# One block for the output norm and the completion of the inverses, bonus loads spread over the chunk steps, and a projection that takes the attention rows first

## What is computed

```python
def encoder_layer(x, p, lambda_init):
    n = rms_norm(x, p['ln1_g'])
    proj = n @ p['w_in']
    rkv = centred_conv(proj[..., :c0], p['conv_rkv'])
    ya = rwkv7_mixer(n, r, k, v, p)              # 8 heads x 64, both directions
    yb = diff_attention(qd, kd, vd, p, lambda_init)  # 4 heads, v 128
    x = x + jnp.concatenate([ya, yb], axis=-1) @ p['w_out']
    n2 = rms_norm(x, p['ln2_g'])
    x = x + (jax.nn.silu(n2 @ p['w_gate']) * (n2 @ p['w_up'])) @ p['w_down']
    return x
# diff_attention ends in: o = rms_norm(o, p['subln_g']) * (1.0 - lambda_init)
# rwkv7_mixer ends in: out = (yn + bonus) * g, yn being y_sum with mean and variance taken per head
```

## Time and profile before

| | us |
|---|---|
| median of 3 runs | 2462.61 (2459.39 to 2468.22) |
| profiled execution, its device time | 2464.25 |
| its span in the profile | 2462.5 |
| TensorE busy | 2185.3 (89%) |
| VectorE busy | 1103.2 (45%) |
| ScalarE busy | 829.2 (34%) |
| GpSimd busy | 349.6 (14%) |

### The profile page before, as it was taken

One profiled execution on the slowest core, in us unless ns is written; L12 is line 12 of the kernel. 1 busy time (PEld: TensorE's weight loads), 2 busy tenths in 40 slices (PEclk: granted clock), 3 DMA queues, 4 the chain that ended last, 5 costly groups with the idle time before them and its releaser, 6 DMA issues. The chain is left out here.

```text
span 2462.5 us, 41471 instructions
## 1 busy us (share of the span) xinstructions
PE 2185.3 (89%) x17078; PEld 1851.3 (75%) x17078; DVE 1103.2 (45%) x1554; ACT 829.2 (34%) x1356; POOL 349.6 (14%) x366
## 2 busy tenths in 40 slices
PE   6999998867397888856999599999999999999999
PEld 5888883344386555546888288999998889999987
DVE  5433006579564777661767544232232222233221
ACT  6111114665374444433445322222222122222211
POOL 0000000000002998043445200000000000000000
PEclk9999999866567999966999799999999999999999
DMA  3222212135693000034784435322223332222232
GB/s 122 89 87 95 80 69 87 51 150 228 232 250 129 1 1 20 33 122 93 187 197 123 145 116 170 103 70 75 77 86 110 120 111 77 77 74 71 76 120 73
DMA packets 133539, 258.47 MB, mean 105 GB/s; under 512 B 10945, under 2 KB 80961, under 8 KB 132129
## 3 DMA queue, kind: packets, MB, share of 16 engines
q1 hardware_dynamic: 133408, 256.63, 32.5%
HBM read 184.69 MB, written 68.93 MB: 103 GB/s over the span
## 5 line engine op out<-in xcount | busy, mean ns | idle before, releaser
L210 PE MATMUL ff_acc<-normed_nh,normed_ff_low 128*128 128x320 f32 x1344 | 416.7, 310 | 6.3 <-SPq L158 5.1
L211 PE MATMUL ff_acc<-normed_nl,normed_ff_high 128*128 128x320 f32 x1344 | 416.3, 310 | 0.0
L212 PE MATMUL ff_acc<-normed_nh,normed_ff_high 128*128 128x320 f32 x1344 | 416.3, 310 | 0.0
L2636 DVE TENSOR_TENSOR normed_ff_low<-normed_ff_raw,normed_ff_high 128x1024 fp32r<-128x1024 f32 x126 | 154.3, 1225 | 427.7 <-ACT normed_ff_high L2600 427.6
L210 PEld LDWEIGHTS ff_acc<-normed_nh,normed_ff_low 128*128 128x128 f32 x1344 | 253.2, 188 | 7.0 <-SPq L158 5.4
L211 PEld LDWEIGHTS ff_acc<-normed_nl,normed_ff_high 128*128 128x128 f32 x1344 | 253.3, 188 | 0.0
L212 PEld LDWEIGHTS ff_acc<-normed_nh,normed_ff_high 128*128 128x128 f32 x1344 | 253.2, 188 | 0.0
L2600 ACT CAST normed_ff_high<-normed_ff_raw 128x1024 fp32r<-128x1024 f32 x126 | 131.8, 1046 | 234.5 <-PE ff_acc L212 233.8
L211 PE MATMUL ff_acc<-normed_ff_low,ff_hh 128*128 128x512 f32 x420 | 163.4, 389 | 0.0
L210 PE MATMUL ff_acc<-normed_ff_high,ff_hl 128*128 128x512 f32 x420 | 163.4, 389 | 0.0
L212 PE MATMUL ff_acc<-normed_ff_high,ff_hh 128*128 128x512 f32 x420 | 163.4, 389 | 0.0
(11 more groups left out here) (321 smaller groups left out, 4287.1 us busy)
## 6 DMA issues: line engine op xcount, KB each, us to landing
dram_sx<-pr_sx SPq DMA_DIRECT2D x8, 2816.0 KB, 8.1
ch_ops<-dram_sx SPq DMA_DIRECT2D x88, 256.0 KB, 4.8
normed_ff_raw<-in_w_gate SPq DMA_DIRECT2D x44, 512.0 KB, 3.3
normed_ff_raw<-in_w_up SPq DMA_DIRECT2D x44, 512.0 KB, 3.3
normed_ff_raw<-in_w_down SPq DMA_DIRECT2D x44, 512.0 KB, 3.6
pj_packed<-in_w_in SPq DMA_DIRECT2D x24, 512.0 KB, 4.5
heads_vt<-dram_sx SPq DMA_DIRECT2D x44, 256.0 KB, 5.4
dram_proj<-pj_mixed SPq DMA_DIRECT2D x12, 656.0 KB, 3.3
```

The costliest lines, as they stand in the source:

```text
L210: nc.tensor.matmul(out, ll, rh, start=start, stop=False)
L211: nc.tensor.matmul(out, lh, rl, start=False, stop=False)
L212: return nc.tensor.matmul(out, lh, rh, start=False, stop=stop)
L2636: nc.vector.tensor_tensor(low[s][:, :], raw[s], high[s][:, :].bitcast(F32), ALU.subtract).then_inc(cut_low[s], 1)
```

## The change

1. `attention_out` and `solve_out` become one block, `attention_out_and_solve_out`. Streams are interleaved: TensorE does a group's first products, a head's ten transposes, the group's second products. `half_ps` and `whole_ps` are single (two banks each), the transposes have three banks, single. The norm's small steps are done for all heads at once. Squares and transposed heads use the room of `y_last`; the attention's `o_rows` and two pairs of buffers of the stage before it lie in `y_first`.
2. The chunk stage's constants (masks, `same`, ident, decay) are loaded in that block, behind the inverses and ahead of the heads' stores. In the chunk stage GpSimd zeroes the state first and the operand slots after it, buffer by buffer; TensorE waits for the zeroing before the first three state products and not before the inner products; SP loads step 2 only after the first state products.
3. The eight bonus loads are issued one each at steps 5, 6, 9, 10, 13, 14, 15 and 16.
4. VectorE adds the bonus of the last three tiles of the mix. The stage doesn't wait for the landing of z; the semaphore lives on, and SP in the projection waits for it before it loads the z rows.
5. The projection loads the first tile's attention rows and its z rows separately, the weights in eight pieces of 512 KB, those for the attention rows first, and multiplies in that order.

```diff
 def attention_out_and_solve_out(nc, g):     # replaces attention_out and solve_out
+        half_ps, whole_ps = (c.ps(n, (P, 2 * 512)) for n in ("half_ps", "whole_ps"))
+        turn_ps = c.ps("turn_ps", (P, 3 * 512))
+        room = g.y_last[:, :, :, :].rearrange("p m e t -> p (m e t)")
+            def _(sp):
+                for grp in range(NG):
+                    sp.dma_start(inv[:, grp, :, :].rearrange("p i j -> p (i j)"),
+                                 g.inverses[:, grp * BLK * BLK:(grp + 1) * BLK * BLK]).then_inc(inv_in[grp], 16)
+                    for q in (1, 3):
+                        sp.dma_start(below[QUADS[q], grp, :, :].rearrange("p u c -> p (u c)"), g.below[q // 2, :, grp]
+                                     ).then_inc(below_in[grp], 16)
+                    if grp == 0:
+                        sp.dma_start(ident[:, :], g.small_of("ident")).then_inc(ident_in, 16)
...
+                for h in range(HEADS):
+                    sp.wait_ge(kept, h + 1)
+                    sp.dma_start(g.mix[RW + h * P:RW + (h + 1) * P, :], oT[h % 2]).then_inc(stored[h % 2], 16)
...
+                sp.wait_ge(chunk_consts, 112)
...
+                sum_up(0)
+                sum_up(1)
+                turn_inverse(0)
+                sum_up(2)
+                sum_up(3)
+                invert()
                 for h in range(HEADS):
+                    turn_inverse(h + 1)
+                    scale(h)
+                turn_inverse(NG - 1)
...
+                first(0)
+                second(0)
+                pe.wait_ge(ident_in, 16)
+                for h in range(HEADS):
+                    first(h + 1)
+                    turn_head(h)
                     if h + 1 < HEADS:
+                        second(h + 1)
+                second(NG - 2)
+                first(NG - 1)
+                second(NG - 1)
...
+                for h in range(HEADS):
+                    square(h)
+                keep_half(0)
+                root()
+                act.wait_ge(gained, 1)
+                keep_whole(0)
+                for h in range(HEADS):
+                    keep_half(h + 1)
+                    keep_head(h)
+                    if h + 1 < HEADS:
+                        keep_whole(h + 1)
+                keep_whole(NG - 2)
+                keep_half(NG - 1)
+                keep_whole(NG - 1)
 
 def chunks_and_mix(nc, g):
+    LATE = TILES - 3
+    BONUS_AT = (5, 6, 9, 10, 13, 14, 15, 16)
...
                 for n in (1, 2):
+                    if n == 2:
+                        for d in both:
+                            sp.wait_ge(bst_done[d], 1)
...
-                    if n == 3 * GS:
+                    if n in BONUS_AT:
+                        i = BONUS_AT.index(n)
+                        k = i // 2
                         for d in both:
-                            sp.wait_ge(u_done[d], n)
...
+                            sp.wait_ge(u_done[d], GS * min(k + 1, 3))
+                        row = (k % 2 * 2 + i % 2) * P + k // 2 * CH
+                        sp.dma_start(g.bon[HALVES[i % 2], k, :], g.bonus[row:row + CH, :]).then_inc(bonus_in, 16)
...
-                sp.wait_ge(stored, 16 * sum(len(runs) for _m, runs in GROUPS))
...
-                pe.wait_ge(zeroed, 1)
                 for p in range(PIECES):
                     inner_products(0, p)
                 for n in range(CHUNKS):
+                    if n < 3:
+                        pe.wait_ge(zeroed, n + 1)
...
-                pool.wait_ge(consts, 96)
                 for d in both:
                     scale_identity(d, 0)
+                for d in both:
+                    nc.gpsimd.memset(vs[0][CHAN[d], d, :, :], 0.0)
                 for s in range(3):
                     for d in both:
-                        nc.gpsimd.memset(ops[s][TOKS[d], :, R_AT[d], :], 0.0)
...
+                        last = nc.gpsimd.memset(ops[s][TOKS[d], :, R_AT[d], :], 0.0)
+                    last.then_inc(zeroed, 1)
...
+                for m in range(LATE, TILES):
+                    dve.wait_ge(gated_y, m + 1)
+                    at = two_chunks(m)
+                    tt(z[:, :, at, :], z[:, :, at, :], bonus[:, :, at, :], ALU.add).then_inc(done_late, 1)
 
 def out_project(nc, g):
+        ORDER = [(b, ks, ks + 2, q) for q, (b, lo) in enumerate(((0, HK), (1, HK), (0, 0), (1, 0))) for ks in (lo, lo + 2)]
...
+                load_m0(FROM_ATTENTION, m0_loaded)
+                weights_part(0)
+                weights_part(1)
                 sp.dma_start(ident[:, :], g.small_of("ident")).then_inc(weights, 16)
...
+                for w in range(2, 5):
+                    weights_part(w)
+                sp.wait_ge(g.z_stored, PRIMED + g.z_stores)
+                load_m0(FROM_Z, m_loaded[0])
+                for w in range(5, 8):
+                    weights_part(w)
                 load_m(1, 1)
```

More of the change, by code:

```diff
@@ L1330, in _ @@
                 total(FIRSTS - 1)
[L1331 removed]
+                for m in range(LATE):
                     pool.wait_ge(gated_y, m + 1)
@@ L2259, in turn @@
                     last.then_inc(turned, 1)
-                product(0, 0, 0, first=True)
+                first_product()
                 with pe.Fori(0, PAIRS - 1) as i:
```

425 lines of the change are left out of this document (201 added, 224 removed).

## The result

The changed kernel takes 2432.86 us (median of four executions, 2423.77 to 2435.84) against 2462.79 for the kernel before, a ratio of 0.987 with a 95% interval of 0.9844 to 0.9897. It is faster, by about 30 us. Two later comparisons of the same two kernels gave 0.9862 (0.9826 to 0.9898) and 0.9873 (0.985 to 0.9896), 34 and 31 us, so 30 to 34 us is what the three together say. The prediction was 2415, a gain of 47.4, and 2430 as the upper end: direction right, size too large, outside its range. The profiled execution took 2435.84 (span 2434.1), the longest of its four.

A forecast was written before the change was run, and what follows sets the result against it. TensorE's last stretch, 1423.7 to 2462.5, bounds the kernel; savings ahead come off one for one. 17.2 + 9.7 + 8.0 + 12.5 = 47.4 off 2464.25 gives 2416.9, as a median 2415 us; range 2405 to 2430.

The forecast's parts named there:

- Part A: Output norm and inverses merged in one block: 61.4 us against 78.6, -17.2, bounds -12.4 and -18.9.
- the 1.7 us for late code: Merged norm and inverses block: allowance for TensorE's code fetch stalls, taken as 1.7 us between bounds 0 and 6.5.
- Part B: Head of the chunk stage, constants and zeroing moved ahead: TensorE starts at 6.1 us instead of 15.8, -9.7.
- Covered, by 1.1; if it isn't, 1 to 2 us: Early chunk steps: held loads land at 21.8 us, wanted at 22.9; if late, 1 to 2 us lost.
- Part C: Chunk steps, bonus loads one a step: -8 us, bounds all 9.1 back or only 5.
- It fits, narrowly, at the four steps that also move y: Chunk steps: a bonus load brings DMA work to 8.1 of 8.4 us, 0.96 of the step.
- Part D: Mix to projection: first DMA 6.0 us earlier, then 6.5 saved to the end of the first product, together -12.5.
- It doesn't do what it says: Rival: a wait for stores or constants still ends last, so the head or projection change gives little; 2426, chance 0.05.
- The long steps were not the bonus loads': Rival, chunk steps: two of three long steps might be code fetch, so spreading gives 1 us; 2422, chance 0.07.
- The bonus spread saturates each step: Rival, chunk steps: operands come late at all eight bonus steps, costing 58 us; slower at 2472, chance 0.02.
- The clock in the first product: Rival, projection: clock stays low, first product runs at half clock, 8.1 us more; 2423, chance 0.10.
- The merged block was not serial: Denies a rival: norm and inverses copies and bursts wait for each other, merging worth only 5 us; 2427, chance 0.10.

The follow-up runs named there:

- its two variants above: Kernel before with only the bonus loads spread one a step, ratio 0.9974; kernel before with only the third step's loads held until the first state products, 1.0019.

## Why the prediction was wrong, point by point

Means over profiles: the kernel before and its two variants above, and the changed kernel with every variant that leaves the stretch alone (for the chunk steps its three profiles and the one with the identity later, against the two of the kernel before).

**What bounds the kernel**: right. 1038.80 us of the end are unchanged.

**Part A** (-17.2, bounds -12.4 and -18.9): the two blocks together took 77.2 to 78.6, the merged one 59.5 to 64.6, on average 63.1 over thirteen profiles: -14.8, within the bounds and 2.4 short. Order and starting point came as worked out; TensorE begins 6.5 us in:

```profile
1064.99 3.62 PE L2067 MATMUL as_half_ps<-as_by_col,as_below 32*32 32x32 f32 x128 [7.08 <-DVE as_by_col L2023]
...
1074.14 0.21 PE L2081 MATMUL as_whole_ps<-as_by_row,as_half 32*32 32x32 f32 x1 [1.24 <-issue]
...
1080.98 1.75 PE L2067 MATMUL as_half_ps<-as_by_col,as_below 32*32 32x32 f32 x58 [3.40 <-issue]
...
1107.20 2.66 PE L2067 MATMUL as_half_ps<-as_by_col,as_below 32*32 32x32 f32 x92 [1.09 <-issue]
```

The step that failed is the 1.7 us for late code, "nearer to none, because TensorE now pauses for data where it used to pause for code". The three waits above are 5.7, and at 3.40 one is longer than the 2.79 of the earlier trace rows; over the thirteen profiles such waits are 4.3 to 9.4 us, 6.4 on average. The pauses for data, 2.2 at most, didn't hide them. The block's own bound of 6.5 was the better value. With it the sum would have been too long, so its other terms had some 3 us too much. They price every burst at the half clock of the earlier trace rows; the granted clock in the merged block was 0.53 to 0.65, and the shortest block had the 0.65.

**Part B** (-9.7): the head took 21.4 to 22.3 and takes 12.5 to 13.6, -8.6 on average. The first inner product came 7.0 us after the stage's start in the first profile, and the forecast was 6.1. Behind it stands the step that cost more. "Covered, by 1.1; if it isn't, 1 to 2 us" asked only whether the held loads bring the *operands* in time, and they did: no wait for an operand stands in the first steps. It was not asked what those loads do to the code packets. The earlier trace rows had already shown such a stall. The first two intervals went from 16.7 to 20.5 to 22.3, +4.8 on average, 2.7 of it shown to be the hold's. By the traces the 4.8 are 3.1 us of waits for nothing and 1.6 of half clock behind them (3.1, 0, 1.7 and 1.6 in the four profiles, counted as half of the time that TensorE worked at 0.50); with the hold in the old kernel it is 2.5 and none. Why the half clock follows in three of these profiles and not in the fourth, whose stop was the 2.93, stays open. The stretch of that step in the first profile:

```profile
1144.58:1158.64 14.06, 11.42 (x191) 10.22 (x193) 6.57 (x21) 4.35 (x12) 4.21 (x5) 0.76 0.92 175
```

0.76 of the full clock on average, 1.00 in the second profile of the same kernel, where the interval took 11.86.

**Part C** (-8, bounds -9.1 and -5): measured alone, -6.4 (-3.5 to -9.4) in time and -3 to -4.5 in the steps; in the changed kernel 4 to 7 against the batch. The reading of the earlier trace rows was right: the batch made those steps long. The term that was mis-sized is "It fits, narrowly, at the four steps that also move y". A share of 0.96 worked out as a mean didn't mean 0.96 in each step. Two intervals of the changed kernel with one load each:

```profile
1202.87:1212.12 9.25, 8.65 (x192) 7.70 (x193) 6.57 (x21) 4.26 (x12) 4.22 (x5) 1.00 1.09 219
1239.10:1248.51 9.41, 8.64 (x193) 7.61 (x193) 6.58 (x21) 4.36 (x12) 4.23 (x5) 1.00 1.08 220
```

1.09 and 1.08, not 0.95 at most, as the change's sign was to be. The first is followed by the 1.47 us stop. Where the same loads stand at steps without y, the excess is 4.5 to 6.4 in three profiles and not 7.3 to 10.4. The reason taken for the near end of the range, "three steps of operands are held ahead", protects against late operands and says nothing of code.

In the nineteen intervals as a whole the changed kernel (mean 168.7 of four profiles) gained 1.9 on the kernel before (170.7) where 8 was due. 3.7 was the spread's worth in the old kernel, so some 2 more are lost between the parts; the batch too is dearer in the changed kernel, 174.3 against 170.7. That the code's place against the loads shifts with every change ahead of it would do this. It was not tested by itself, and the cause of these 2 us stays open.

**Part D** (-12.5): the first DMA came 5.6 us earlier after the last step's products (6.0 forecast), and from there to the next stage it is 160.5 to 161.7 in place of 166.3, -5.1 (6.5 forecast). Together -10.7. The rows landed as worked out, the attention rows 3.0 after the first DMA (2.8), the first piece at 4.3 (4.2):

```profile
1373.36 0.38 SPq L2205 DMA_DIRECT2D op_m<-dram_mix  x1
...
1376.36 0.62 ACT L2329 CAST op_m_high<-op_m 128x512 fp32r<-128x512 f32 x1 [14.53 <-DMA op_m<-dram_mix]
...
1377.67 1.04 ACT L2325 CAST op_w_high<-normed_ff_raw 128x1024 fp32r<-128x1024 f32 x1 [0.69 <-DMA normed_ff_raw<-in_w_out]
...
1381.30 1.04 ACT L2325 CAST op_w_high<-normed_ff_raw 128x1024 fp32r<-128x1024 f32 x1 [2.59 <-DMA normed_ff_raw<-in_w_out]
...
1381.53 0.80 PE L210 MATMUL op_acc<-op_w_high,op_m_low 128*128 128x512 f32 x1 [17.55 <-DMA op_ident<-in_small]
```

What failed is "the pieces come every 1.35 us": the second came 3.6 after the first. The identity, whose load moved from first to fourth of the queue, held the product back to 8.2, a wait that the prediction overlooked; the experiment shows that it costs nothing, as the second piece is later still.

**Sum**: -14.8 -8.6 +2.9 (steps) -10.7 = -31.2, beside 30 to 34 measured. Short of the forecast are 2.4 + 1.1 + 10.9 + 1.8 = 16.2, two thirds of them in the chunk steps. These exceed 21 times 8.42 by 13.4 us: 8.5 of waits for nothing, 2.4 of half clock behind them and 2.5 of other. In the kernel before it was 10.5: 7.4, 2.2 and 0.9. The forecast took 8 of these away; the change left as much late code as it found. The step that failed is thus the one behind both B and C: loads held back or spread were priced by whether their operands come in time and whether a mean share stays under 1, and what they do to TensorE's code was put at nothing.

The bounds of the range don't add up as stated: the four terms above the forecast (+4.8, +2.4, +3 and 3.4 for D's start) give 2429, without the last 2425, and not 2424.

**Rivals.** "It doesn't do what it says" falls. "The long steps were not the bonus loads'" named the code as the cause in place of the loads; the runs show both in one, code made late by the loads. "The bonus spread saturates each step" was given 0.02 as a loss of 58 us: the share did pass 1.0 at two or three of the eight, at less than a tenth of that price, because TensorE there waited for one packet of code and not for its operands. The clock in the first product was 0.80 and not low throughout. The merged block was not serial. No rival had code made late by the change's own loads, though a row of late code stood in part A; that is why the range ended at 2430.

The Trainium skill (Runtime: NRT & Kernel Launch, Instruction fetch mechanics) says that code is streamed in blocks of 16 KB by a DMA queue and that crossing a block is mostly hidden. The size agrees with the trace (94 packets, 1.54 MB), and so does "mostly": 34 packets in the chunk steps left ten waits or fewer. As a rule to plan with it doesn't hold beside full queues, where single waits came to 3.8 us.

## What to carry to other kernels

Loads that bring every operand in time can still make an engine's code late; look for waits that end by nothing shown, in the middle of a run of equal instructions, and for the distance of the packets in the instruction queue. Before loads are moved or spread, write down the DMA share of each step that they go to and not a mean: here loads of 1.6 us cost nothing that shows at shares of 0.6 to 0.7 and 2 to 5 us in all where they took some steps over 1. When several parts of a change fill idle time of the same resource, don't add up their gains unchecked: here the spread was worth 3.7 us by itself in the later steps, which gained 1.9 with the whole change.

An edit that moves loads to other steps of a queue's program need not move them so in time. The loads written for steps 18, 19 and 20 all left together, because SyncE's queue first waits for the buffer of the last operand loads, three steps ahead, and after that the loads' own waits were met or nearly so. The trace shows it and the edit doesn't.

## What the runs showed of the hardware that was not expected

A wait for code follows the loads to wherever they are put: 3.57 us at the batch's place, 3.77 with the batch at the end of the steps, 1.6 to 2.9 for the longest where held loads meet the second step, and 4.9 us in all when fewer loads are let go at once.

Such a stop is often paid for twice. Of 23 stops of 1.8 to 3.8 us inside the steps of the 17 profiles, 18 were followed by 3.4 or 6.8 us at a granted clock of 0.50.

VectorE was slowed in the merged block, where GpSimd copies in SBUF beside it. Three of four scalings of the same shape took longer, 1.82 to 2.10 us in all thirteen profiles with this block, than the 1.43 to 1.49 of the kernel before, whose norm had no GpSimd work beside it; the transposes between them, with one input, did not. VectorE and then GpSimd, of the changed kernel:

```profile
1075.03 1.45 DVE L2042 TENSOR_TENSOR first_y_first<-first_y_first,as_st 128x1280 f32<-128x1280 f32 x1
...
1078.18 1.91 DVE L2024 STREAM_TRANSPOSE as_by_row<-as_inv 128x1024 f32<-128x1024 f32 x1
1079.94 2.01 DVE L2042 TENSOR_TENSOR first_y_first<-first_y_first,as_st 128x1280 f32<-128x1280 f32 x1
...
1085.55 1.88 DVE L2042 TENSOR_TENSOR first_y_first<-first_y_first,as_st 128x1280 f32<-128x1280 f32 x1
```
```profile
1078.50 2.12 POOL L2013 COPY rows_est<-as_by_row 32x1024 f32<-32x1024 f32 x2
1080.67 3.25 POOL L2013 COPY rows_est<-as_by_col 32x1024 f32<-32x1024 f32 x2
```

The Trainium skill (SBUF — State Buffer, Who interferes with whom) has it that an instruction of VectorE with two inputs in SBUF contends with a GpSimd instruction that reads SBUF, and one with a single input, outside some faster modes, doesn't. The trace agrees: 2.01 and 1.88 against 1.45 for the one that began ahead of GpSimd's next copy, and 1.91 unchanged for the single input. It cost nothing here, as VectorE is busy for 36.65 of the block's 63.9 us.
